# The 640 token columns of each matrix product cut as 512 and 128 instead of 256 and 384

## The chip, the cores and the metric

The kernel runs on one core of a Trainium2 chip. The metric is the device time of one execution in microseconds (us). Two executions of the kernel before took 2782.54 and 2783.83 us, median 2783.18 us.

## The reference, cut to what matters

The kernel computes one inference step of a small transformer-like trunk: four layers over 512 sample tokens and 128 prompt tokens (640 in all), model width 1024. A layer is a token mixer and a gated feed-forward network:

```python
for i in range(DEPTH):                       # 4 layers: conv, pool, attention, conv
    hp = modulate(rms_norm(xp, norm1_w[i]), mod_p[0], mod_p[1])   # 128 prompt tokens
    hs = modulate(rms_norm(xs, norm1_w[i]), mod_s[0], mod_s[1])   # 512 sample tokens
    mp, ms = mixer(hp), mixer(hs)            # short conv / pooling / attention
    xp, xs = xp + mod_p[2] * mp, xs + mod_s[2] * ms
    hp = modulate(rms_norm(xp, norm2_w[i]), mod_p[3], mod_p[4])
    hs = modulate(rms_norm(xs, norm2_w[i]), mod_s[3], mod_s[4])
    xp = xp + mod_p[5] * swiglu(hp, ffn_in_w[i], ffn_out_w[i])    # 1024 -> 2x2816 -> 1024
    xs = xs + mod_s[5] * swiglu(hs, ffn_in_w[i], ffn_out_w[i])
```

Both groups of tokens use the same weights, but have modulation vectors of their own. Nearly all the arithmetic is in the products with the weight matrices, in float32 accuracy.

## The kernel before, in words

**Layout.** Features lie on the 128 partitions, tokens along the free axis: a row of 640 columns holds the 512 sample tokens and then the 128 prompt tokens. Each product's input is kept as two rows of the reduced type float32r, a rounded high part and the remainder (`h_hi`, `h_lo` for the normed stream with two more columns for the two shift vectors, so 642 columns; `g_hi`, `g_lo` for the gated rows, 640 columns). Each 128-wide block of output features is a *unit*: its weights (128 x 1024 float32) are loaded by DMA into `raw`, ScalarE rounds them into `w_hi` (L593), VectorE makes the remainder `w_lo` (L841).

**A unit on TensorE** is in `products` (L371 to L394). For each of 8 (or 6, or 2) input blocks `k` there are three passes, `w_hi` with the high row, `w_hi` with the low row, `w_lo` with the high row. Each pass is two matmuls with the same 128x128 weights: one over the first `TA` token columns into PSUM bank `2*slot` (L392), one over the others into bank `2*slot+1` (L393). This text calls these two a *pair*. A PSUM bank holds 512 float32 columns, and the two slots alternate from unit to unit. Each matmul instruction brings its own weight load (LDWEIGHTS in the trace), also where the weights are those of the matmul before.

**After a unit**, VectorE reads the sums out of PSUM with the views `sample_of` and `prompt_of`: `scaled_out` (L907) copies the two shift columns and multiplies with the inverse norm, `out_quad` (L940) adds into the residual `x`. Sample and prompt are separate instructions already, for each has its own factor. Then `freed` lets TensorE use the slot again, two units later.

**Order.** Each engine runs its own program; semaphores tie them. ScalarE's and VectorE's split of the weights for a unit two ahead follows the end of a unit (`step`). SyncE issues the weight loads, each waiting for `raw` to come free; GpSimd issues the loads of the modulation weights, which VectorE sums in gaps. Where a row of the next product is made from the units just done (end of a feed-forward chunk, a norm), TensorE waits per block `k` for `g_ready` or `h_ready`.

**Other users of `TA`.** The sums of squares over features (`sum_features`, `sum_squares`, `head_sums`, L420 to L455) are plain float32 matmuls with a matrix of ones, cut at `TA` into the two banks of `ps_sum`; ScalarE reads the two banks with two square roots cut at the same place (L659, L660, L721, L722).

Of the kernel before, what the change touches and what calls it, by code (L numbers as in the profile page):

```python
# [28 lines left out]
TS = 512  # L29
TP = 128  # L30
# [10 lines left out]
WINDOWS = (2, 4, 8, 16)  # L41
NMOD = 6

TA = 256

Q_ZU, Q_B, Q_OUT, Q_QKV, Q_IN, Q_LAST = 4, 2, 2, 3, 4, LAST // 2
Q_FFN = 2 * (Q_IN + Q_OUT) + Q_LAST + Q_OUT
# [37 lines left out]
def build(nc, d):  # L85
    with ExitStack() as ctx:
# [39 lines left out]
        ps = ctx.enter_context(nc.psum_tensor("ps", [P, 4, 512], F32))  # L126
# [93 lines left out]
        block = ctx.enter_context(nc.Block())  # L220

        def sample_of(slot):
            return ps[:, 2 * slot:2 * slot + 2, 0:TA]

        def prompt_of(slot):
            return ps[:, 2 * slot + 1, TA:TA + TP]

        def at_(index):

            return slice(index, index + 1) if isinstance(index, int) else bass.ds(index, 1)  # L230

        def halves(row):
            return row.rearrange("p (b n) -> p b n", b=2)

        def parts(slot, row, off_s=0, off_p=TS):

            return ((sample_of(slot), halves(row[:, off_s:off_s + TS])),
                    (prompt_of(slot), row[:, off_p:off_p + TP]))

        def groups(row):  # L240
# [129 lines left out]
        def _(pe):  # L370
            def products(q, j, a_hi, a_lo, tiles, width=T, ready=None, norm=None):  # L371
# [6 lines left out]
                for k in range(tiles):  # L378
# [11 lines left out]
                    for n, (w, a) in enumerate(passes):  # L390
                        begin, end = k == 0 and n == 0, k == tiles - 1 and n == 2
                        pe.matmul(ps[:, 2 * slot, 0:TA], w[:, slot, ws], a(k)[:, 0:TA], start=begin, stop=end)  # L392
                        mm = pe.matmul(ps[:, 2 * slot + 1, 0:width - TA], w[:, slot, ws], a(k)[:, TA:width], start=begin, stop=end)  # L393
                mm.then_inc(unit_done, 1)  # L394
# [22 lines left out]
            def sum_features(src, s, value, done):  # L417

                pe.wait_ge(s, value)
                pe.matmul(ps_sum[:, 0, 0:TA], ones[:], src[:, 0:TA], start=True, stop=True)  # L420
                pe.matmul(ps_sum[:, 1, 0:T - TA], ones[:], src[:, TA:T], start=True, stop=True).then_inc(done, 1)

# [414 lines left out]
        def _(dve):  # L837
# [69 lines left out]
            def scaled_out(q, j, row, off_s=0, off_p=TS):  # L907

                slot = j % 2
                dve.tensor_copy(bias[:, j, :], ps[:, 2 * slot + 1, T - TA:TH - TA])  # L910
                for (src, dst), (_, r) in zip(parts(slot, row, off_s, off_p), parts(slot, rinv)):
                    v = dve.tensor_tensor(dst, src, r, ALU.mult)  # L912
                v.then_inc(freed[slot], 1)

                dve.wait_ge(freed[slot], evacuated(q, j))
# [24 lines left out]
            def out_quad(q, m0, n, gate, tiles, squares, folds=True, ada=None, triples=1):  # L940


                for j in range(4):
                    m = m0 + j
                    late = squares and m == KD - 1
                    if not late:
                        step(q, j, tiles[j])
                    else:
                        dve.wait_ge(unit_done, 4 * q + (j + 1))
                    for g, (src, dst) in enumerate(parts(j % 2, x[:, m, :]) if isinstance(m0, int) else  # L950
                                                   dynamic_parts(j % 2, m)):
                        v = dve.scalar_tensor_tensor(out=dst, in0=src, scalar=gate(m, g), in1=dst,
                                                     op0=ALU.mult, op1=ALU.add)
                    v.then_inc(freed[j % 2], 1)
                    if squares:
                        if folds:

                            dve.wait_ge(freed[j % 2], evacuated(q, j))
                        if m >= 2:
                            add_square(m - 1, n)  # L960
                        if late:
                            add_square(m, n)
                        if folds:
                            fold_lo(m, n)
                    if late:
                        step(q, j, tiles[j])
                    if triples == 1:
                        ada_in_step(ada, j)
                    else:
                        ada_twice(ada, j)  # L970
# [15 lines left out]
            def dynamic_parts(slot, m):  # L986
                row = x[:, bass.ds(m, 1), :].rearrange("p a t -> p (a t)")
                return parts(slot, row)
# [437 lines left out]
```

## Time and profile before

| | |
|---|---|
| median of two executions | 2783.18 us |
| span of the profiled execution | 2781.9 us |
| its mean granted TensorE clock | 0.987 of full speed |
| TensorE matmul busy | 2684.9 us, 97% |
| TensorE weight loads busy | 2615.1 us, 94% |
| VectorE busy | 1756.1 us, 63% |
| ScalarE busy | 858.9 us, 31% |
| GpSimd busy | 103.3 us, 4% |
| DMA, mean over the span | 105 GB/s |

The profiled execution is one run of the program recorded by the hardware profiler; its span is from the first to the last instruction. Busy time is the union of an engine's instructions. Matmuls overlap in the records, since each is shown from its issue to the end of its drain, so the mean duration of a matmul is more than its share of the engine's time: what it costs is read from one start to the next.

### The profile page before, as it was taken

How to read it: one execution, taken by the hardware profiler on the slowest of the kernel's cores; microseconds unless marked ns; L12 is line 12 of the kernel's file. 1: busy time of each engine (PE TensorE's matmuls, PEld its weight loads, DVE VectorE, ACT ScalarE, POOL GpSimd, SP SyncE). 2: the span in 40 equal slices, each digit the busy share in tenths (PEclk: the TensorE clock that was granted, in tenths of full speed). 3: DMA queues.
4: the chain of work that ended last, by engine and by line, in shares of the span. 5: the costliest groups of instructions: out<-in, count | busy, mean ns of one | idle time of the engine just before them, and what ended most of it. 6: DMA issues, size and time to landing. Idle time of an engine off the chain costs nothing.

```text
span 2781.9 us, 46075 instructions
## 1 busy us (share of the span) xinstructions
PE 2684.9 (97%) x17562; PEld 2615.1 (94%) x17562; DVE 1756.1 (63%) x3033; ACT 858.9 (31%) x1174; POOL 103.3 (4%) x199
## 2 busy tenths in 40 slices
PE   7998999999969999999988999999999999999997
PEld 7998999999959999999954999999999999999996
DVE  6888868775587776746665477767465554334344
ACT  3222332322343223124345332231242233223122
POOL 1000000000000000000000000000000000000000
PEclk9999999999979999999999999999999999999998
DMA  7344335343113443412100334434122222222221
GB/s 281 129 139 147 128 125 178 128 159 106 47 52 129 143 157 131 151 66 80 50 1 0 114 129 144 160 127 151 66 78 76 76 68 76 76 76 74 70 68 61
DMA packets 84442, 293.31 MB, mean 105 GB/s; under 512 B 9984, under 2 KB 12416, under 8 KB 84224
## 3 DMA queue, kind: packets, MB, share of 16 engines
q1 hardware_dynamic: 58000, 196.09, 21.0%
q0 software_dynamic: 26352, 95.96, 10.2%
q8 instruction: 64, 1.05, 0.2%
q14 instruction: 26, 0.21, 0.0%
HBM read 289.13 MB, written 2.88 MB: 105 GB/s over the span
## 4 chain that ended last, share of the span: by engine, by line
PE 89%; DVE 6%; ACT 2%; issue 2%; DMA 1%; DVEq 0%; ACTq 0%; POOL 0%; POOLq 0%
PE ps L393 50%; PE ps L392 34%; PE ps_x L500 1%; PE ps L479 1%; DVE w_lo L841 1%; DVE tmp L912 1%; ACT w_hi L593 1%; DVE g_lo L855 1%; DVE tmp L920 1%; DMA ada_w<-in_ada_w 1%; PE ps_sum L490 0%; DVE ps_x L869 0%; ACT tmp L734 0%; ACT g_hi L605 0%; DVE mix L1102 0%
## 5 line engine op out<-in xcount | busy, mean ns | idle before, releaser
L841 DVE TENSOR_TENSOR w_lo<-raw,w_hi 128x1024 fp32r<-128x1024 f32 (+2 forms) x364 | 431.0, 1184 | 696.1 <-ACT w_hi L593 692.2
L593 ACT ACTIVATE w_hi<-raw 128x1024 fp32r<-128x1024 f32 (+2 forms) x364 | 373.3, 1026 | 947.8 <-PE ps L393 947.2
L393 PE MATMUL ps<-h_lo,w_hi 128*128 128x386 f32 x1904 | 651.4, 342 | 0.0
L393 PE MATMUL ps<-h_hi,w_hi 128*128 128x386 f32 x1904 | 648.6, 341 | 0.0
L393 PE MATMUL ps<-h_hi,w_lo 128*128 128x386 f32 x1904 | 646.5, 340 | 0.0
L392 PE MATMUL ps<-h_hi,w_hi 128*128 128x256 f32 x1904 | 545.7, 287 | 22.5 <-DVE h_lo L976 15.6
L392 PE MATMUL ps<-h_hi,w_lo 128*128 128x256 f32 x1904 | 535.8, 281 | 0.0
L392 PE MATMUL ps<-h_lo,w_hi 128*128 128x256 f32 x1904 | 535.5, 281 | 0.0
L869 DVE CUSTOM_DVE_ANT_0 ps_x<-ada_w,cond 128x1024 f32<-128x1024 f32 x366 | 450.6, 1231 | 47.2 <-DVE tmp L912 16.4
L392 PEld LDWEIGHTS ps<-h_hi,w_hi 128*128 128x128 f32 x1904 | 360.6, 189 | 28.9 <-DVE h_lo L976 13.6
L393 PEld LDWEIGHTS ps<-h_hi,w_hi 128*128 128x128 f32 x1904 | 361.2, 190 | 3.0 <-issue 2.0
L392 PEld LDWEIGHTS ps<-h_hi,w_lo 128*128 128x128 f32 x1904 | 363.7, 191 | 0.0
L392 PEld LDWEIGHTS ps<-h_lo,w_hi 128*128 128x128 f32 x1904 | 362.2, 190 | 0.0
L393 PEld LDWEIGHTS ps<-h_hi,w_lo 128*128 128x128 f32 x1904 | 361.7, 190 | 0.0
L393 PEld LDWEIGHTS ps<-h_lo,w_hi 128*128 128x128 f32 x1904 | 360.1, 189 | 0.0
L393 PE MATMUL ps<-g_hi,w_hi 128*128 128x384 f32 x896 | 303.4, 339 | 0.0
L393 PE MATMUL ps<-g_lo,w_hi 128*128 128x384 f32 x896 | 303.4, 339 | 0.0
L393 PE MATMUL ps<-g_hi,w_lo 128*128 128x384 f32 x896 | 303.2, 338 | 0.0
L392 PE MATMUL ps<-g_hi,w_hi 128*128 128x256 f32 x896 | 252.3, 282 | 11.0 <-DVE g_lo L855 9.0
L392 PE MATMUL ps<-g_lo,w_hi 128*128 128x256 f32 x896 | 250.6, 280 | 0.0
L392 PE MATMUL ps<-g_hi,w_lo 128*128 128x256 f32 x896 | 250.5, 280 | 0.0
L912 DVE TENSOR_TENSOR tmp<-ps,tmp 128x512 f32<-128x512 f32 x448 | 196.4, 480 | 0.0
(123 smaller groups left out, 2735.0 us busy)
## 6 DMA issues: line engine op xcount, KB each, us to landing
raw<-in_weights SPq DMA_DIRECT2D x324, 512.0 KB, 3.2
ada_w<-in_ada_w POOLq DMA_DIRECT2D x183, 512.0 KB, 3.5
raw<-in_weights SPq DMA_DIRECT2D x32, 384.0 KB, 2.9
mix<-in_ada_head SPq DMA_DIRECT2D x9, 512.0 KB, 8.5
x<-in_x SPq DMA_DIRECT2D x4, 640.0 KB, 9.7
out_y<-mix SPq DMA_DIRECT2D x8, 320.0 KB, 2.2
cond<-in_cond SPq DMA_DIRECT2D x1, 1024.0 KB, 4.8
raw<-in_weights SPq DMA_DIRECT2D x8, 128.0 KB, 2.3
```

The source lines that it names most:

```text
L392: pe.matmul(ps[:, 2 * slot, 0:TA], w[:, slot, ws], a(k)[:, 0:TA], start=begin, stop=end)
L393: mm = pe.matmul(ps[:, 2 * slot + 1, 0:width - TA], w[:, slot, ws], a(k)[:, TA:width], start=begin, stop=end)
L479: pe.matmul(out[:, 0:TS], row[:, qt * P:(qt + 1) * P], key[:, 0:TS], start=True, stop=True)
L500: pe.matmul(ps_rot, val, of_sample[:, k, :], start=(k == 0), stop=(k == 4))
L593: act.activation(w_hi[:, j % 2, 0:tiles * P], raw[:, j, 0:tiles * P], ACT.Copy).then_inc(w_hi_ready, 1)
L841: dve.tensor_tensor(w_lo[:, j % 2, 0:tiles * P], raw[:, j, 0:tiles * P], w_hi[:, j % 2, 0:tiles * P].bitcast(F32), ALU.subtract).then_inc( ...
L855: dve.tensor_tensor(g_lo[:, index, :], src, g_hi[:, index, :].bitcast(F32), ALU.subtract).then_inc(g_ready, 1)
L869: dve.tensor_tensor_reduce(ada_products, ada_w[:, j * D:(j + 1) * D], cond[:, v, :], 1.0, 0.0, ALU.mult, ALU.add, ada_raw[:, j, v:v + 1]). ...
L912: v = dve.tensor_tensor(dst, src, r, ALU.mult)
L920: v = dve.scalar_tensor_tensor(out=row[:, at:at + n], in0=row[:, at:at + n], scalar=bias[:, j, g:g + 1], in1=other[:, o:o + n], op0=ALU.ad ...
```

## The change

`TA`, the place of the cut, goes from 256 to 512. The first matmul of a pair then has 512 columns (all sample tokens, one full bank), the second has 128 columns, or 130 with the shift columns. The PSUM views follow: the sample sums are one bank instead of two half banks, the prompt sums start at column 0 of the other bank instead of 256, and the helper that folded a row into two halves goes. All expressions in `TA` follow, those of the sums of squares and of the square roots too. No instruction is added or taken away, and no wait is changed.

```diff
-TA = 256
+TA = 512
...
         def sample_of(slot):
-            return ps[:, 2 * slot:2 * slot + 2, 0:TA]
+            return ps[:, 2 * slot, 0:TS]
 
         def prompt_of(slot):
-            return ps[:, 2 * slot + 1, TA:TA + TP]
+            return ps[:, 2 * slot + 1, 0:TP]
...
-        def halves(row):
-            return row.rearrange("p (b n) -> p b n", b=2)
-
         def parts(slot, row, off_s=0, off_p=TS):
 
-            return ((sample_of(slot), halves(row[:, off_s:off_s + TS])),
+            return ((sample_of(slot), row[:, off_s:off_s + TS]),
                     (prompt_of(slot), row[:, off_p:off_p + TP]))
```

## Rows read from the trace of the kernel before

**Rows 1.** The page: busy time, granted clock in 40 slices, chain of waits.
```profile
PE 2684.9 (97%) x17562; PEld 2615.1 (94%) x17562; DVE 1756.1 (63%) x3033; ACT 858.9 (31%) x1174; POOL 103.3 (4%) x199
...
PEclk9999999999979999999999999999999999999998
...
PE 89%; DVE 6%; ACT 2%; issue 2%; DMA 1%; DVEq 0%; ACTq 0%; POOL 0%; POOLq 0%
```

**Rows 2.** The page, costliest groups: one of three rows of each kind of product.
```profile
L393 PE MATMUL ps<-h_hi,w_hi 128*128 128x386 f32 x1904 | 648.6, 341 | 0.0
L392 PE MATMUL ps<-h_hi,w_hi 128*128 128x256 f32 x1904 | 545.7, 287 | 22.5 <-DVE h_lo L976 15.6
...
L393 PE MATMUL ps<-g_hi,w_hi 128*128 128x384 f32 x896 | 303.4, 339 | 0.0
L392 PE MATMUL ps<-g_hi,w_hi 128*128 128x256 f32 x896 | 252.3, 282 | 11.0 <-DVE g_lo L855 9.0
```

**Rows 3.** Busy time by stretch: length, engines' busy (x instructions), granted clock, DMA.
```profile
400.00:570.00 170.00, 169.88 (x1149) 169.62 (x1148) 127.13 (x217) 49.51 (x56) 12.67 (x24) 1.00 0.45 148
2240.00:2400.00 160.00, 160.00 (x1080) 159.51 (x1079) 78.38 (x126) 60.81 (x78) 0.00 (x0) 1.00 0.22 73
```

**Rows 4.** Chain of waits inside a unit: start, us to the next start, what.
```profile
1250.57 0.18 PE ps L393
1250.75 0.12 PE ps L392
1250.87 0.18 PE ps L393
1251.05 0.12 PE ps L392
```

**Rows 5.** Timeline, matmuls (PE) and weight loads (PEld): start, us, what.
```profile
2689.99 0.28 PE L392 MATMUL ps<-h_hi,w_hi 128*128 128x256 f32 x1
2689.99 0.19 PEld L393 LDWEIGHTS ps<-h_hi,w_hi 128*128 128x128 f32 x1
2690.11 0.34 PE L393 MATMUL ps<-h_hi,w_hi 128*128 128x386 f32 x1
2690.11 0.19 PEld L392 LDWEIGHTS ps<-h_lo,w_hi 128*128 128x128 f32 x1
2690.28 0.28 PE L392 MATMUL ps<-h_lo,w_hi 128*128 128x256 f32 x1
```

**Rows 6.** Timeline of TensorE: plain float32 matmuls of 1, 2, 128 and 512 columns.
```profile
38.89 1.84 PE L550 MATMUL ps<-cond_k,mix 128*128 128x2 f32 x16
40.59 0.68 PE L428 MATMUL ps_sum<-tmp,ones 128*128 128x256 f32 x2
...
1404.79 1.28 PE L459 MATMUL ps_sum<-ones,tmp 128*128 128x1 f32 x10 [2.04 <-ACT tmp L729]
1405.93 1.10 PE L467 MATMUL ps_x<-mix,turn 128*128 128x512 f32 x2
...
1427.50 0.38 PE L480 MATMUL ps<-ada_w,tmp 128*128 128x128 f32 x2
1427.72 3.60 PE L500 MATMUL ps_x<-ada_w,tmp 128*128 128x512 f32 x8
1431.16 1.02 PE L500 MATMUL ps_x<-ada_w,cache_v 128*128 128x512 f32 x2
```

**Rows 7.** Groups by shape, weight loads of float32r and of plain float32 matmuls.
```profile
L392 PEld LDWEIGHTS ps<-h_hi,w_lo 128*128 128x128 f32 x1904 | 363.7, 191 | 0.0
L459 PEld LDWEIGHTS ps_sum<-ones,tmp 128*128 128x128 f32 x80 | 10.0, 191 | 2.2 <-ACT tmp L729 2.2
```

**Rows 8.** Who TensorE waited for before L392: us, times (all its causes).
```profile
  DVE h_lo L976: 29.2, 5
  DVE g_lo L855: 22.7, 19
```

**Rows 9.** Groups by shape on VectorE: reads of PSUM and the weight split.
```profile
L841 DVE TENSOR_TENSOR w_lo<-raw,w_hi 128x1024 fp32r<-128x1024 f32 x324 | 396.9, 1225 | 629.5 <-ACT w_hi L593 625.7 <-DVE tmp L1007 2.0 <-issue 1.4
L912 DVE TENSOR_TENSOR tmp<-ps,tmp 128x512 f32<-128x512 f32 x224 | 152.4, 680 | 0.0
L1167 DVE TENSOR_TENSOR ps_x<-ps_x,rope 128x512 f32<-128x512 f32 x10 | 7.0, 698 | 1.5 <-PE ps_x L467 1.2
```

## The prediction

> **What bounds the kernel.** I read the page first: TensorE is busy 97% of the span, 89% of the chain of waits is TensorE, and its granted clock is 1.00 almost everywhere [rows 1]. VectorE has slack even in its fullest steady stretch (127 of 170 us) and half its time in a late one (78 of 160 us), while TensorE is busy the whole of both [rows 3]. So the time is a number of matmuls times their spacing. The count comes from the page: three rows with 1904 and three with 896 for each of L392 and L393, so 3 x 1904 + 3 x 896 = 8400 pairs [rows 2]. The spacing can't be taken from the mean durations (287 and 341 ns overlap); it is read from a stretch without waits: 160 us with 1080 matmuls, 148.1 ns each or **296.3 ns a pair** [rows 3]. 8400 x 0.2963 = 2489 us of the 2781.9 us span. The chain splits the pair: about 0.12 us from a 256-column start to the next, about 0.18 us from a 384- or 386-column start [rows 4].
>
> A pair moves 642 columns 5712 times and 640 columns 2688 times, 641.4 on average. At the granted 1.00, the 2.4 GHz level, one column a cycle would be 267.2 ns. The measured pair is 29.1 ns longer. Both pieces show this in proportion (0.12 us for 256, 0.18 for 386), so I book 0.462 ns a column.
>
> The view that decides is the timeline with weight loads. The load for the next matmul starts when the current matmul starts (L393's at 2689.99, with the 256-column matmul; L392's at 2690.11, with the 386-column one) and the next matmul starts after it [rows 5]. One load runs ahead, never two. So the spacing behind a matmul is the longer of its own columns and the load of the next weights. Today both matmuls are long enough to cover a load.
>
> **The change part by part.** *The large piece.* 512 columns by 0.462 ns is 236.5 ns. If instead the excess is fixed per matmul (29.1 / 2 = 14.5 ns), it is 213.3 + 14.5 = 227.8 ns. I take 236.5, since the 256- and 386-column pieces both fit the rate, and keep 227.8 as the lower bound. The load for the small piece is well covered here.
>
> TensorE: Matmul & The Clock Gate (the Trainium skill), section "Back-to-back issue gap", gives N / 2.4 + 2.5 ns, an estimate of 215.8 ns for 512; the trace disagrees for these products, since it would make a 386-column gap 163 ns where the chain shows 0.18 us. With it the sum below would be some 174 us less.
>
> *The small piece.* 128 or 130 columns alone would be 60 ns at the booked rate, but beneath it must run the load for the next 512-column matmul. No short float32r matmul is in the trace, so the load's length is bounded by neighbours. Sixteen 2-column matmuls take 40.59 - 38.89 = 1.70 us, 0.106 us each; ten 1-column records take 1405.93 - 1404.79 = 1.14 us, 0.114 us each; two 128-column plain float32 records take 0.22 us, 0.11 us each [rows 6]. The first two have nearly nothing to move, so this is the load. The load records of float32r and plain float32 have the same length, 191 ns [rows 7], which speaks for the same load. From above it is bounded by the 256-column spacing, about 0.118 us (the 296.3 ns pair shared by columns), within which a float32r load fits today. I take the middle, **0.112 us**, between 0.106 and 0.118.
>
> *The pair after* is 236.5 + 112 = 348.5 ns, 52.2 ns more, and 8400 x 0.0522 = **+438 us**. It lies wholly on TensorE, which has no slack in the steady stretches. Of what the change adds in the stretches where TensorE waits, a little is absorbed: waits for the last gated row are 22.7 us in 19, for the last normed row 29.2 us in 5 [rows 8]. TensorE runs up to 5 to 7 blocks of three pairs before such a wait, each now 0.16 us longer, so 0.8 to 1.1 us goes where the wait is that long. Most of the 19 are shorter; seven such reliefs give **-7 us** (bounds 0 and -24, all 24 waits at a full us).
>
> *Sums of squares and head sums.* Plain float32: a 512-column record takes 3.44 / 8 = 0.43 us, a 128-column one 0.11 us [rows 6], that is 0.84 and 0.86 ns a column, so cutting 640 columns elsewhere costs nothing on these matmuls. Their load is covered even under 128 columns at this slower pace.
>
> *VectorE's and ScalarE's reads.* Sample sums come from one bank instead of two halves: 680 ns today for 512 columns over two banks; 698 ns for 512 columns of one bank in the rotary product, which also writes to PSUM [rows 9]. Between -20 and +20 ns a read, hidden under a unit of 24 pairs (7.1 us now, 8.4 us after). If it were exposed it would be so only at the 24 places above, under 1 us in all. The square roots move the same columns. Cost zero. The weight split (1225 ns per unit [rows 9]) and the DMAs keep their work and get 18% more time, so no engine becomes a new bound, and nothing new is queued on SP or GpSimd.
>
> *Sum:* the profiled 2781.9 + 438 - 7 = 3213 us; the median of the runs lies 1.3 us above that span, so 3214, which I state as **3215 us**. Its own range: 334 ns a pair with both lower bounds (+316 - 24, 3075 us) to 354.5 ns (+489, 3272), widened to 3290 in case the load also suffers from the fast streaming.
>
> **The rivals.** *1. The load is short for float32r, and hides.* If the 0.106 to 0.118 us floor belongs to plain float32 alone, the small piece costs its 60 ns and the pair is (512 + 129.4) x 0.462 = 296.3 ns as before: 2783 us, no change. The place is L393's gap; it decides when the load is under 60 ns. For it: the trace only bounds a float32r load from above. Against it: equal load records [rows 7]. TensorE: Matmul & The Clock Gate (the Trainium skill), section "Weight-path perf modes", says that a fast weight load is on for 128 columns where the type isn't FP32, with no win for 4-byte weights; whether float32r counts as FP32 there is what this rival turns on. Chance 0.08. With it, the 29 ns excess could belong to loads starving the stream and shrink under the long piece: at most 267.2 ns a pair, 244 us less, 2539 us; chance 0.03.
>
> *2. In between.* The load is 60 to 100 ns, so the pair is 297 to 334 ns with either price of the large piece: 2790 to 3075 us. The same page of the Trainium skill, section "Back-to-back issue gap", has about 81 ns for a sustained 128-column stream with loads, an estimate of 317.5 ns a pair and 2961 us; the rows of very short matmuls here stay at 0.106 us or more [rows 6]. Chance 0.06.
>
> *3. A short float32r matmul falls back to the pace of plain float32.* A plain matmul appears as two records, 0.22 us in all for 128 columns [rows 6]. If the array needs a long stream to run float32r at one column a cycle, the small piece costs 218 ns, the pair 454.5 ns: +158.2 ns x 8400 = +1329 us, 4104 us. For it: every float32r product in the trace has at least 256 columns [rows 2], so nothing shows the fast pace below. Against it: the two records of a plain matmul are passes over parts of the operands, and nothing in the rows ties the number of passes to length. Chance 0.16.
>
> **How the numbers follow.** Load floor as worked out 0.67, short load 0.08, short load with gain 0.03, in between 0.06, plain pace 0.16. The likeliest case's own range is 3075 to 3290; to hold 8 in 10 the range must take in the cheaper side, down to no change: 0.67 + 0.06 + 0.08 = 0.81, so 2780 to 3290. The plain pace stays outside. Two per cent is about what a measurement of this kernel can tell from no change; faster 0.03, within 0.08, slower 0.89.
>
> **What would show it.** In the changed profile: the same 17562 matmuls; in a steady stretch 174 ns a matmul; in the chain L392 pieces of 0.23 to 0.24 us and L393 pieces of 0.11 to 0.12 us; the load of L392 starting with L393's matmul and filling its gap; VectorE busy as before in us. L393 at 0.06 us means rival 1, at 0.22 us rival 3, or two records for each. It would be wrong in size if the 512-column gap is near 0.215 us. A stretch in which VectorE or a DMA ends the wait would mean that I missed a cause.

## The result and the profile after

The changed kernel takes 3164.99 us (two executions, 3163.09 and 3166.88 us) against 2783.18 us before: 1.1369 times as long, 95% interval 1.1351 to 1.1388. That is 382 us more, where 432 were forecast. The page of the changed kernel, whose line numbers are three lower than before (L389 is now the first matmul of a pair, L390 the second), answers to [rows 1, 2]:

```profile
span 3160.9 us, 46075 instructions
...
PE 3078.2 (97%) x17562; PEld 2648.2 (84%) x17562; DVE 1758.7 (56%) x3033; ACT 860.0 (27%) x1174; POOL 103.7 (3%) x199
...
PEclk9999999999989999999999999999999999999998
...
PE 94%; DVE 3%; ACT 1%; DMA 1%; issue 1%; ACTq 0%; DVEq 0%; POOL 0%; POOLq 0%
...
L389 PE MATMUL ps<-h_hi,w_hi 128*128 128x512 f32 x1904 | 852.6, 448 | 18.7 <-DVE h_lo L973 14.2
...
L390 PE MATMUL ps<-h_hi,w_hi 128*128 128x130 f32 x1904 | 426.8, 224 | 0.0
```

The same number of instructions and the same 17562 matmuls, at the same granted clock. VectorE and ScalarE do the same microseconds of work as before (1758.7 and 860.0), and the span is longer by 379.0 us, nearly all of it TensorE's (3078.2 - 2684.9 = 393.3 us busy). So the matmuls stand farther apart. The steady stretch, in the view of busy time by stretch (length, then busy us and instructions of each engine, granted clock, DMA share and GB/s):

```profile
2560.00:2720.00 160.00, 160.00 (x931) 139.70 (x930) 67.22 (x110) 51.73 (x65) 0.00 (x0) 1.00 0.18 63
```

931 matmuls in 160 us are 171.9 ns each, **343.7 ns a pair**, where [rows 3] had 296.3. The 47.4 ns more, 8400 times, are 398 us.

Where in the pair they lie can be read in two ways, and the two seem to disagree. The chain of waits (start, us to the next step) puts them in the long matmul:

```profile
2500.43 0.28 PE ps L389
2500.71 0.06 PE ps L390
2500.77 0.28 PE ps L389
2501.06 0.06 PE ps L390
```

Against [rows 4], the short piece takes 0.06 us, what its columns need, and the long one 0.28 us, more than its columns at any rate seen before. The timeline with the weight loads (PEld) of the same stretch reads otherwise:

```profile
2500.20 0.23 PE L390 MATMUL ps<-h_lo,w_hi 128*128 128x130 f32 x1
2500.21 0.19 PEld L389 LDWEIGHTS ps<-h_hi,w_lo 128*128 128x128 f32 x1
2500.27 0.44 PE L389 MATMUL ps<-h_hi,w_lo 128*128 128x512 f32 x1
2500.32 0.19 PEld L390 LDWEIGHTS ps<-h_hi,w_lo 128*128 128x128 f32 x1
2500.55 0.23 PE L390 MATMUL ps<-h_hi,w_lo 128*128 128x130 f32 x1
2500.55 0.19 PEld L389 LDWEIGHTS ps<-h_hi,w_hi 128*128 128x128 f32 x1
2500.61 0.45 PE L389 MATMUL ps<-h_hi,w_hi 128*128 128x512 f32 x1
```

The load for the long matmul starts with the short one, at 2500.21, and the next load (L390's) only at 2500.32: 0.11 us for a load. (The load records are 0.19 us long and overlap each other; their spacing is read here, not their length.) Then 0.23 us pass to the load at 2500.55, which is the long matmul's streaming. The long matmul is stamped as started at 2500.27, when the short one's columns are through. If only one load runs ahead, its weights are in only at 2500.32, when the next load starts. Read from load to load the pair is 0.11 + 0.23, as forecast; read from matmul to matmul it is 0.06 + 0.28. The experiments had to tell which of the two is at work.

### The profile page after: what moved, and what is told of

It is laid out like the page before. It is cut to its first block, busy times and chain, and to the rows that moved or that the text cites. A ratio compares the mean times of both kernels' runs of the same rounds, so it can differ in the third digit from the quotient of the medians.

```text
span 3160.9 us, 46075 instructions
## 1 busy us (share of the span) xinstructions
PE 3078.2 (97%) x17562; PEld 2648.2 (84%) x17562; DVE 1758.7 (56%) x3033; ACT 860.0 (27%) x1174; POOL 103.7 (3%) x199
## 4 chain that ended last, share of the span: by engine, by line
PE 94%; DVE 3%; ACT 1%; DMA 1%; issue 1%; ACTq 0%; DVEq 0%; POOL 0%; POOLq 0%
PE ps L389 74%; PE ps L390 16%; PE ps_x L497 1%; PE ps L476 1%; DMA ada_w<-in_ada_w 0%; PE ps_sum L487 0%; PE ps_sum L425 0%; PE ps_x L464 0%; ACT tmp L731 0%; DMA mix<-in_ada_head 0%; DVE mix L1099 0%; DVE tmp L1004 0%; PE ps_sum L456 0%; DVE h_lo L973 0%; PE ps L547 0%
## 5 line engine op out<-in xcount | busy, mean ns | idle before, releaser
L389 PE MATMUL ps<-h_hi,w_hi 128*128 128x512 f32 x1904 | 852.6, 448 | 18.7 <-DVE h_lo L973 14.2
L389 PE MATMUL ps<-h_lo,w_hi 128*128 128x512 f32 x1904 | 852.3, 448 | 0.0
L389 PE MATMUL ps<-h_hi,w_lo 128*128 128x512 f32 x1904 | 849.1, 446 | 0.0
L389 PEld LDWEIGHTS ps<-h_hi,w_hi 128*128 128x128 f32 x1904 | 360.5, 189 | 103.7 <-DVE h_lo L973 11.8
L389 PEld LDWEIGHTS ps<-h_hi,w_lo 128*128 128x128 f32 x1904 | 362.0, 190 | 83.9
L389 PEld LDWEIGHTS ps<-h_lo,w_hi 128*128 128x128 f32 x1904 | 361.2, 190 | 83.0
L390 PE MATMUL ps<-h_lo,w_hi 128*128 128x130 f32 x1904 | 429.0, 225 | 0.0
L390 PE MATMUL ps<-h_hi,w_hi 128*128 128x130 f32 x1904 | 426.8, 224 | 0.0
L390 PE MATMUL ps<-h_hi,w_lo 128*128 128x130 f32 x1904 | 426.7, 224 | 0.0
L389 PE MATMUL ps<-g_hi,w_hi 128*128 128x512 f32 x896 | 396.6, 443 | 1.7 <-DVE g_lo L852 1.7
L389 PE MATMUL ps<-g_hi,w_lo 128*128 128x512 f32 x896 | 396.5, 442 | 0.0
L389 PE MATMUL ps<-g_lo,w_hi 128*128 128x512 f32 x896 | 396.4, 442 | 0.0
L390 PEld LDWEIGHTS ps<-h_hi,w_hi 128*128 128x128 f32 x1904 | 366.0, 192 | 1.7 <-issue 1.7
L390 PEld LDWEIGHTS ps<-h_hi,w_lo 128*128 128x128 f32 x1904 | 366.4, 192 | 0.0
L390 PEld LDWEIGHTS ps<-h_lo,w_hi 128*128 128x128 f32 x1904 | 365.5, 192 | 0.0
L389 PEld LDWEIGHTS ps<-g_hi,w_hi 128*128 128x128 f32 x896 | 168.2, 188 | 39.2 <-DVE g_lo L852 2.8
L390 PE MATMUL ps<-g_hi,w_lo 128*128 128x128 f32 x896 | 199.6, 223 | 0.0
L390 PE MATMUL ps<-g_lo,w_hi 128*128 128x128 f32 x896 | 199.5, 223 | 0.0
L390 PE MATMUL ps<-g_hi,w_hi 128*128 128x128 f32 x896 | 199.5, 223 | 0.0
```

## The experiments

The theories, the first three of which come near the 343.7 ns: **load floor** (a load of 0.11 us must run beneath the short matmul), **long matmul slow by itself** (0.28 us for 512 columns, as the chain has it), **half pace** (a float32r matmul under 256 columns at two cycles a column, 0.107 us for 128), and for the sweep **plain pace** (four cycles a column: a short float32r matmul as slow as a plain float32 one).

### wide192: a longer second matmul, still under the load

```diff
+BEG = 448
...
-                        mm = pe.matmul(ps[:, 2 * slot + 1, 0:width - TA], w[:, slot, ws], a(k)[:, TA:width], start=begin, stop=end)
+                        mm = pe.matmul(ps[:, 2 * slot + 1, 0:width - BEG], w[:, slot, ws], a(k)[:, BEG:width], start=begin, stop=end)
```

(and `prompt_of` and the bias copy start 64 columns further on.)

> The changed kernel, but the second matmul of each pair covers 192 columns (194 with the shifts), the last 64 sample tokens once more beside the prompt tokens; nobody reads the repeated columns. Load floor (the load of the next weights, about 0.11 us, must run beneath the second matmul; 192 columns are 0.088 us, still less): pair unchanged at 0.3435 us, 3165 us. Long matmul slow by itself (0.283 us as its start gap shows, the second by its columns): 0.283 + 0.088 = 0.371 us, +27.5 ns x 8400 = +231, 3396 us. Short float32r matmuls at half pace below 256 columns: 0.232 + 0.160 = 0.392 us, +407, 3572 us.

Measured: 3169.95 us, 1.1389 times before (1.137 to 1.1408), 5 us from the changed kernel. 64 more columns in each of 8400 matmuls cost next to nothing. Slow long matmul and half pace, which wanted 3396 and 3572 us, fall. In its chain of waits the short matmul has grown to 0.09 us and the long one (L390 there) has shrunk from 0.28 to 0.25 us, with the same 512 columns:

```profile
2300.02 0.09 PE ps L391
2300.11 0.25 PE ps L390
```

### wide256: the second matmul just covers the load

The same edit with `BEG = 384`.

> The same with 256 columns (258 with the shifts) in the second matmul, 128 sample tokens repeated. Load floor: the second matmul now just covers the load, 0.118 us, pair 0.232 + 0.118 = 0.350 us, +55, 3220 us. Long matmul slow by itself: 0.283 + 0.118 = 0.401 us, +483, 3648 us. Half pace below 256 columns: 256 is not below, so 3220 us as with the load floor.

Measured: 3240.14 us, 1.1639 (1.162 to 1.1659), 75 us above the changed kernel where 55 were expected. Another 64 columns now cost 70 us, 8 ns a pair: the matmul has grown out of the load's cover. The chain of waits of this kernel has the long matmul (L390 again) at 0.23 to 0.24 us, though nothing about it changed:

```profile
2299.85 0.24 PE ps L390
2300.09 0.12 PE ps L391
2300.21 0.23 PE ps L390
```

So the 0.28 us was never the price of 512 columns.

### cut448: each column once, 448 and 192

```diff
-                        pe.matmul(ps[:, 2 * slot, 0:TA], w[:, slot, ws], a(k)[:, 0:TA], start=begin, stop=end)
-                        mm = pe.matmul(ps[:, 2 * slot + 1, 0:width - TA], w[:, slot, ws], a(k)[:, TA:width], start=begin, stop=end)
+                        pe.matmul(ps[:, 2 * slot, 0:CUT], w[:, slot, ws], a(k)[:, 0:CUT], start=begin, stop=end)
+                        mm = pe.matmul(ps[:, 2 * slot + 1, 0:width - CUT], w[:, slot, ws], a(k)[:, CUT:width], start=begin, stop=end)
...
-            return ((sample_of(slot), row[:, off_s:off_s + TS]),
+            return ((sample_of(slot), row[:, off_s:off_s + CUT]),
+                    (ps[:, 2 * slot + 1, 0:TS - CUT], row[:, off_s + CUT:off_s + TS]),
```

> Each pair cut as 448 and 192 columns (194 with the shifts), no column twice; VectorE reads the sample sums in two pieces, 448 and 64. Sums of squares stay cut at 512. Load floor: 448 x 0.455 = 0.204, plus 0.111 for the load, 0.315 us, -28.5 ns x 8400 = -239, about 2926 us. Long matmul slow by its columns (0.283 / 512 each): 0.248 + 0.088 = 0.336 us, about 3102 us. Half pace below 256: 0.204 + 0.160 = 0.364 us, about 3337 us.

Measured: 2940.61 us, 1.0564 (1.0546 to 1.0581), 14 us from the load floor's 2926 and 160 or more from the others. Moving 64 columns from the long matmul, where each costs time, to the short one, where the load hides them, gives back 224 us.

### small_first: the order of the two

```diff
-                        pe.matmul(ps[:, 2 * slot, 0:TA], w[:, slot, ws], a(k)[:, 0:TA], start=begin, stop=end)
-                        mm = pe.matmul(ps[:, 2 * slot + 1, 0:width - TA], w[:, slot, ws], a(k)[:, TA:width], start=begin, stop=end)
+                        pe.matmul(ps[:, 2 * slot + 1, 0:width - TA], w[:, slot, ws], a(k)[:, TA:width], start=begin, stop=end)
+                        mm = pe.matmul(ps[:, 2 * slot, 0:TA], w[:, slot, ws], a(k)[:, 0:TA], start=begin, stop=end)
```

> The changed kernel with the two matmuls of a pair in the other order, 128 (130) columns first and 512 after. Load floor: each short matmul still has one load beneath it, the next long one's, so the pair stays 0.3435 us and the time 3165 us; the start gaps stay 0.28 us behind the long and 0.06 us behind the short one, whichever is called first. If instead the cost hung on reloading the same weights right behind a long matmul or on the order of the banks, the time would move by up to 8400 x 0.05 = 400 us.

Measured: 3155.39 us, 1.1336 (1.1317 to 1.1355), 10 us or 0.3% under the changed kernel, nothing of the up to 400 us. Its long matmul, now called second, still has 0.28 us in the chain. The order is not the cause; where the 10 us come from stays open.

### cut384 and cut320: both long enough

The edit of cut448 with `CUT = 384` and `CUT = 320`.

> Each pair cut as 384 and 256 columns (258 with the shifts), the kernel before in the other order of sizes; VectorE reads the sample sums in pieces of 384 and 128. Load floor: both matmuls cover a load, so a pair costs its columns, 0.296 us, 2783 us. Long matmul slow by its columns (0.283 / 512 each beyond 386?): at most 0.213 + 0.119 = 0.332 us, 3084 us. The third VectorE read per unit is hidden: no part of the time.

> Each pair cut evenly, 320 and 320 columns (322 with the shifts); VectorE reads the sample sums in pieces of 320 and 192. Load floor: 0.296 us a pair, 2783 us, no gain over 256 and 384, for the load is already covered there. If the excess of 0.029 us a pair over one column a cycle came from the 256-column matmul only just covering its load, the pair would fall towards 0.28 us, -137, 2646 us.

Measured: 2781.82 us, 0.9991 (0.9981 to 1.0) and 2790.19 us, 1.0024 (1.0014 to 1.0034). Both agree with columns alone, to 0.3%. The slow long matmul's 3084 us is refuted once more, and the hoped-for 2646 us at 320 is not there: the kernel before is not held up by its 256-column matmul. The additional VectorE read in both (364 more instructions) does not show in the time, as expected.

One late stretch of each kernel, in the order before, cut384, cut320, cut448, the changed kernel, wide192, wide256, small_first, shows the pair without its surroundings:

```profile
2600.00:2700.00 100.00, 100.00 (x678) 100.00 (x678) 37.31 (x65) 22.21 (x27) 0.00 (x0) 1.00 0.21 71
```

```profile
2600.00:2700.00 100.00, 100.00 (x680) 100.00 (x679) 38.87 (x82) 22.86 (x28) 0.00 (x0) 1.00 0.21 70
```

```profile
2600.00:2700.00 100.00, 100.00 (x678) 100.00 (x677) 36.77 (x73) 21.46 (x26) 0.00 (x0) 1.00 0.22 72
```

```profile
2600.00:2700.00 100.00, 100.00 (x635) 95.10 (x633) 39.03 (x83) 35.43 (x41) 0.00 (x0) 1.00 0.20 69
```

```profile
2600.00:2700.00 100.00, 100.00 (x580) 86.99 (x579) 39.45 (x66) 31.27 (x38) 0.00 (x0) 1.00 0.20 67
```

```profile
2600.00:2700.00 100.00, 100.00 (x581) 86.80 (x580) 40.46 (x67) 33.12 (x41) 0.00 (x0) 1.00 0.19 63
```

```profile
2600.00:2700.00 100.00, 100.00 (x566) 86.75 (x565) 45.05 (x67) 32.17 (x46) 0.00 (x0) 1.00 0.18 62
```

```profile
2600.00:2700.00 100.00, 100.00 (x585) 87.25 (x584) 38.94 (x71) 31.34 (x37) 0.00 (x0) 1.00 0.19 63
```

The first count after the length is TensorE's busy time with its matmuls: 200 us divided by it is the pair. That gives 0.295, 0.294, 0.295, 0.315, 0.345, 0.344, 0.353 and 0.342 us. With 640 columns in all the pair is flat where both matmuls have 256 or more and longer once one is shorter. With 512 in the long one it is flat from 128 to 192 in the short one, and longer again at 256.

### sums_only: the other users of the cut

In the kernel before, `TA` becomes `TS` (512) in the sums of squares and the square roots alone:

```diff
-                pe.matmul(ps_sum[:, 0, 0:TA], ones[:], src[:, 0:TA], start=True, stop=True)
+                pe.matmul(ps_sum[:, 0, 0:TS], ones[:], src[:, 0:TS], start=True, stop=True)
```

> The kernel before with only the sums of squares and their square roots cut at 512 and 128, the products as before at 256. Expected by all theories: no change, within 3 us of 2783, as plain float32 matmuls take 0.84 to 0.86 ns a column at either size.

Measured: 2783.11 us, 0.9997 (0.9987 to 1.0006). That part of the change costs nothing, and the products carry all of it.

### sweep: the matmuls by themselves

```diff
             sum_features(sq_sum, sq_added, (KD - 1) * (2 * DEPTH + 1), sum_ready)
+            pe.wait_ge(freed[0], 2 * QUADS + 1)
+            pe.wait_ge(freed[1], 2 * QUADS + 1)
+            for sizes in ((512,), (448,), (384,), (320,), (256,), (192,), (128,), (64,), (2,), (512, 128), (384, 256), (512, 256)):
+                for r in range(32 // len(sizes)):
+                    for s, n in enumerate(sizes):
+                        pe.matmul(ps_x[:, s, 0:n], w_hi[:, 0, 0:P], h_hi[:, 0, 0:n], start=True, stop=True)
```

> The changed kernel, and behind the last sum on TensorE rows of float32r matmuls back to back with the same weights, 32 each of 512, 448, 384, 320, 256, 192, 128, 64 and 2 columns, then alternating 512/128, 384/256 and 512/256; their results are not used. Load floor: start to start 0.23 us at 512, falling with the columns to about 0.11 us at 256 or a little below, and flat at 0.107 to 0.112 us for 192, 128, 64 and 2; alternating 0.343 us a pair for 512/128, 0.296 for 384/256, 0.35 for 512/256. Long matmul slow: 0.28 us at 512 alone, 0.06 us at 128 alone. Half pace below 256: 0.16 us at 192, 0.107 at 128, 0.053 at 64. Plain pace at short lengths: 0.32 at 192, 0.21 at 128.

All these rows have one source line and melt into one in the timeline. The stretches (first fence) give the granted clock, the chain of waits (second fence: start, us in all, number of matmuls) the spacing. The granted clock fell near the end of the 64-column row, stood at 0.50 through the 2-column row and was back at 1.00 before the row alternating 512 and 128 columns ended:

```profile
3184.00:3190.00 6.00, 6.00 (x44) 6.00 (x43) 0.00 (x0) 0.00 (x0) 0.00 (x0) 0.74 0.00 0
3187.00:3194.50 7.50, 7.50 (x38) 7.50 (x37) 0.00 (x0) 0.00 (x0) 0.00 (x0) 0.50 0.00 0
3201.00:3206.90 5.90, 5.90 (x40) 5.64 (x40) 0.00 (x0) 0.00 (x0) 0.00 (x0) 1.00 0.01 3
```

```profile
3187.18 7.21 PE ps_x L589 x34
3200.99 2.06 PE ps_x L589 x12
3203.46 3.44 PE ps_x L589 x24
```

At the granted 0.50, the 1.2 GHz level, 34 matmuls (the first few of 64 columns, the others of 2) take 7.21 us, 0.212 us each: nearly twice the 0.111 us that sweep2 shows at 1.00. So the floor goes with this clock and is no fixed time. At 1.00 again, 12 matmuls alternating between 512 and 128 columns take 2.06 us, **0.343 us a pair**: the pair of the changed kernel, with VectorE and ScalarE idle. 24 matmuls alternating between 384 and 256 columns take 3.44 us, 0.287 us a pair, some 8 ns less than the 0.295 us of the kernels with 640 columns and a cut at 384 or 256. The next run, sweep2 (one execution, like sweep), gives each row a line of its own.

### sweep2: half the weights

```diff
+            for _ in range(32):
+                pe.matmul(ps_x[0:128, 0, 0:128], w_hi[:, 0, 0:128], h_hi[:, 0, 0:128], start=True, stop=True)
...
+            for _ in range(32):
+                pe.matmul(ps_x[0:64, 0, 0:128], w_hi[:, 0, 0:64], h_hi[:, 0, 0:128], start=True, stop=True)
```

> The changed kernel with rows of matmuls behind the last sum on TensorE, each row on a line of its own, 32 matmuls back to back, results not used: float32r of 512, 384, 256, 240, 224, 192, 128 and 64 columns with all 128 weight columns, and of 512, 256, 128 and 64 with only 64 weight columns, 128 with 32; then bfloat16 of 512, 256 and 128 columns with 128 weight columns. If the floor of 0.112 us under short matmuls is the load of the weights, half the weight columns halve it: 128 columns then cost their own 0.059 us, 64 columns about 0.056 us, and the knee at full weights lies near 0.112 / 0.458 = 245 columns (240 columns 0.112, 256 columns 0.118 us). If it is a fixed least time of any float32r matmul, it stays at 0.112 us with 64 and 32 weight columns. Whether the long matmul's 0.234 us (0.213 at one column a cycle) comes from the load that runs beneath it: then 512 columns with 64 weight columns fall to about 0.224 us; if from float32r streaming itself they stay at 0.234, and bfloat16 takes about 0.215 us.

Its timeline of TensorE (start, us until the last one's end, 32 matmuls a row; 128*64 is a load of 64 weight columns):

```profile
3156.85 7.46 PE L590 MATMUL ps_x<-g_hi,w_hi 128*128 128x512 f32 x32
3164.15 5.78 PE L592 MATMUL ps_x<-h_hi,w_hi 128*128 128x384 f32 x32
3169.76 3.95 PE L594 MATMUL ps_x<-h_hi,w_hi 128*128 128x256 f32 x32
3173.55 3.74 PE L596 MATMUL ps_x<-h_hi,w_hi 128*128 128x240 f32 x32
...
3180.69 3.72 PE L600 MATMUL ps_x<-h_hi,w_hi 128*128 128x192 f32 x32
3184.25 3.71 PE L602 MATMUL ps_x<-h_hi,w_hi 128*128 128x128 f32 x32
3187.80 4.04 PE L604 MATMUL ps_x<-h_hi,w_hi 128*128 128x64 f32 x32
...
3200.44 7.51 PE L608 MATMUL ps_x<-h_hi,w_hi 128*64 128x512 f32 x32
3207.78 3.90 PE L610 MATMUL ps_x<-h_hi,w_hi 128*64 128x256 f32 x32
3211.51 2.08 PE L612 MATMUL ps_x<-h_hi,w_hi 128*64 128x128 f32 x32
3213.43 2.00 PE L614 MATMUL ps_x<-h_hi,w_hi 128*64 128x64 f32 x32
3215.27 7.67 PE L616 MATMUL ps_x<-h_hi,w_hi 128*128 128x512 f32 x32
3222.78 2.08 PE L618 MATMUL ps_x<-h_hi,w_hi 128*32 128x128 f32 x32
3224.69 7.65 PE L620 MATMUL ps_x<-h_hi,w_hi 128*128 128x512 f32 x32
3232.41 6.85 PE L622 MATMUL ps_x<-h_hi,w_hi 128*128 128x512 bf16 x31
3239.10 3.66 PE L624 MATMUL ps_x<-h_hi,w_hi 128*128 128x256 bf16 x32
3242.59 1.95 PE L626 MATMUL ps_x<-h_hi,w_hi 128*128 128x128 bf16 x32
3244.47 1.97 PE L628 MATMUL ps_x<-h_hi,w_hi 128*64 128x128 bf16 x32
```

From one row's start to the next, divided by 32: 0.228 us for 512 columns, 0.175 for 384, 0.118 for 256, 0.112 for 240 (the row behind it starts at 3177.13); then 0.111 for 192 ((3184.25 - 3180.69) / 32) and 0.111 for 128: the floor. With 64 weight columns, 64 moving columns take (3215.27 - 3213.43) / 32 = **0.058 us**, about twice what 64 columns need at the rate of the long ones and half the floor of 0.111. 128 moving columns take (3213.43 - 3211.51) / 32 = 0.060 us, and the same with 32 weight columns, (3224.69 - 3222.78) / 32, so there they pay for their columns alone. Halving the weights halves the floor, and neither a least time of a float32r matmul nor a slow pace of short ones does that. The long matmul hardly cares: 512 columns with 64 weight columns (3207.78 - 3200.44) / 32 = 0.229 us, against (3222.78 - 3215.27) / 32 = 0.235 us with 128, the boundaries of the rows included, and 0.228 us in the first row.

Fewer weight columns also mean fewer rows of results. The bfloat16 rows speak against that as the cause: they give all 128 rows of results with no such floor. 512 columns take (3239.10 - 3232.41) / 31 = 0.216 us (31 records are in the trace), 256 columns 0.109 us, and 128 columns (3244.47 - 3242.59) / 32 = 0.059 us with all 128 weight columns, the boundary to the next row included. Inside the 128-column row 22 matmuls take 1.23 us, 0.056 us each:

```profile
3242.98 1.23 PE ps_x L626 x22
```

## Why the prediction was right, and what it missed

**The bound and the count.** Right: TensorE's spacing times 8400 pairs. All of the change is in it. sums_only shows the sums of squares at zero. VectorE's read of the sample sums was also rightly put at nothing: 681 ns from one bank against 680 from two.

**The small piece** (0.112 us, from the 1-, 2- and 128-column rows [rows 6]). Right: 0.111 us in sweep2, and shown to be the load by halving the weights (0.058 us). Plain float32 rows were a good stand-in for float32r here.

**The large piece** was the mis-sized term: 0.2365 us was taken from 0.462 ns a column of the average pair; the pair less the floor is 343.7 - 111 = 232.7 ns, wide256's chain has 0.23 to 0.24, sweep2 0.228 to 0.235 us. The pair came out at 343.7 instead of 348.5 ns, and 8400 x 4.8 = 40 us of the miss of 50 are here. The fixed excess per matmul, the lower bound (0.2278 us), was as near as the rate. TensorE: Matmul & The Clock Gate (the Trainium skill), section "Back-to-back issue gap", has N / 2.4 + 2.5 ns. The bfloat16 rows of sweep2 agree (0.109 us for 256 columns against 0.1092), the float32r rows do not (0.175 us for 384 against 0.1625).

**The absorption** was put at 7 us and is 14 to 19: TensorE's idle time in the span fell from 97.0 to 82.7 us, and 398 us by the pairs stand against 379.0 in the span. Who TensorE waited for ahead of L389:

```profile
  DVE h_lo L973: 25.9, 5
  ...
  DVE g_lo L852: 4.5, 8
```

Against [rows 8] the waits for the last gated row went from 22.7 us in 19 to 4.5 us in 8, those for the last normed row from 29.2 to 25.9 us. I had relieved seven waits; eleven of the 19 gated ones went, and the eight left are short.

**Rivals.** The short load that hides (no change, 2783 us) is refuted for float32r by the floor of sweep2, and with it the chance of a gain (2539 us): cut320, where both matmuls cover the load with room, takes 2790 us. The load in between (60 to 100 ns, 2790 to 3075 us) is refuted by the same 0.111 us. The same page of the Trainium skill, section "Weight-path perf modes", makes a fast load depend on the type not being FP32, and the rows agree, if float32r counts as FP32: floor 0.111 us in float32r, and a 128-column bfloat16 matmul at 0.059 us (0.056 inside the row) with the same 128 weight columns. The plain pace (4104 us) is refuted by wide192 and sweep2: 192 and 128 columns cost the same, and 128 columns cost 0.060 us as soon as the load is short.

**The marker failed.** I had written that L393 at 0.06 us would mean the hidden load, and the chain does show 0.06 us. By that line alone the right theory would have been dropped. The pair's sum was the safe reading. The place of the stall in it depends on whether a matmul's stamp waits for its weights, and here it does not: with 128, 192 and 256 columns in the short matmul the long one's 512 columns show as 0.28, 0.25 and 0.23 to 0.24 us, while the pair stays at 0.344 to 0.345 us in the first two.

## What to carry to other kernels

With a weight load in front of each float32r matmul, at the granted clock of 1.00, a matmul costs the longer of its columns and the next load: about 0.45 to 0.46 ns a column, at least 0.11 us for 128 weight columns. The knee lies near 245 columns (240 columns take 0.112 us, 256 take 0.118). Cut a row so that no piece falls under it; any cut above is as good as another (256, 320 and 384 of 640 columns agree within 0.3%), and the number of VectorE's reads of PSUM costs nothing beside it (364 more in cut384 and cut320). No run left out the second load of a pair, which brings the weights of the first once more; whether that would lift the floor is not shown. Where a stall could sit in either of two neighbouring records, sum them, and find the place by changing one of them.

## What was not expected of the hardware

- A float32r matmul takes 0.175 us for 384 columns, 9 to 10% over one column a cycle at 2.4 GHz, with VectorE and ScalarE idle behind the end of the kernel, and a 512-column one takes nearly the same with 64 weight columns as with 128. A bfloat16 one takes 0.109 us for 256 and 0.216 for 512. At the granted 0.50 the excess is not there: in sweep2's 512-column row behind the 64-column one (granted 0.50 from 3192.30 to 3194.10) the starts of matmuls three apart are at 3192.22 and 3193.51, that is 1.29 us, 0.43 us each, which is one column a cycle at 1.2 GHz. What in the type costs this stays open. In the kernel it is about 29 ns in each pair, and no cut touches it; in sweep's row of 384 and 256 columns it is about 20 ns, and why the kernel's pair has more stays open too.
- After rows of short matmuls TensorE's granted clock fell although matmuls followed each other without a gap: 0.74 in the stretch with 64- and 2-column rows of sweep, 0.50 from 3187.00 to 3194.50. It was back at 1.00 by 3201, in the row alternating 512 and 128 columns.
